# The gated linear attention of a hybrid decoder layer: from 32-token chunks to 128-token chunks by block levels

## The reference

```python
b = jnp.cumsum(gc, axis=1)                       # log decay, per token and key channel
diff = b[:, :, None] - b[:, None, :]
decay = jnp.exp(jnp.where(causal, diff, -jnp.inf))
att = jnp.einsum('bthd,bshd,btshd->bhts', qc, kc, decay)
o = einsum('bhts,bshv->bthv', att, vc) + einsum('bthd,bhdv->bthv', qc * exp(b), S)
S = S * exp(b_last)[..., None] + einsum('bshd,bshv->bhdv', kc * exp(b_last - b), vc)
```

## Time and profile before

| | us |
|---|---|
| median of three runs (lowest to highest) | 2495.36 (2492.14 to 2497.21) |
| the profiled execution's own time | 2494.72 |
| its span in the trace | 2492.9 |
| mean granted TensorE clock | 0.976 |

### The profile page before, as it was taken

The page is one execution under the profiler, slowest core; times in us unless marked ns, Lnnn a source line. Parts: engine busy times, 40 slices in busy tenths (PEclk is TensorE's granted clock), DMA queues, the critical chain, the costliest instruction groups (busy, mean ns, idle before and its releaser), DMA issues.

```text
span 2492.9 us, 47167 instructions
## 1 busy us (share of the span) xinstructions
PE 2452.3 (98%) x19106; PEld 2385.9 (96%) x19106; DVE 1360.8 (55%) x1555; ACT 989.3 (40%) x1037; POOL 162.2 (7%) x182
## 2 busy tenths in 40 slices
PE   8999999999999999999999999999999999999997
PEld 8999999999999998898888989999999999999997
DVE  6555554554556545544565465655555555555554
ACT  5333333333333334454455543444333333333332
POOL 0000000000004200010000130020000000000015
PEclk9999999999999999987898999999999999999998
DMA  5445445444444443251121544454445445445444
GB/s 210 168 152 185 168 157 182 168 167 167 183 170 151 176 163 131 102 192 69 67 81 71 188 176 169 169 185 170 184 164 191 184 166 189 183 167 189 184 166 139
DMA packets 67109, 401.72 MB, mean 161 GB/s; under 512 B 8706, under 2 KB 11426, under 8 KB 31696
## 3 DMA queue, kind: packets, MB, share of 16 engines
q1 hardware_dynamic: 62960, 386.86, 43.4%
q0 software_dynamic: 4080, 13.88, 1.6%
HBM read 391.43 MB, written 9.27 MB: 161 GB/s over the span
## 4 chain that ended last, share of the span: by engine, by line
PE 93%; DVE 2%; issue 2%; ACT 1%; POOL 1%; DMA 0%; DVEq 0%; SPq 0%; ACTq 0%; POOLq 0%
PE bank L1345 29%; PE bank L1351 29%; PE bank L1346 28%; PE bank L386 1%; PE bank L407 1%; PE bank L425 1%; ACT w_hi L618 1%; DVE w_lo L946 1%; PE bank L1479 0%; PE bank L423 0%; PE bank L370 0%; POOL scratch L596 0%; PE bank L1586 0%; PE bank L1477 0%; PE bank L1537 0%
## 5 line engine op out<-in xcount | busy, mean ns | idle before, releaser
L618 ACT ACTIVATE w_hi<-raw 128x2048 fp32r<-128x2048 f32 (+1 forms) x404 | 705.4, 1746 | 1238.0 <-PE bank L1351 1194.6
L946 DVE TENSOR_TENSOR w_lo<-raw,w_hi 128x2048 fp32r<-128x2048 f32 (+1 forms) x404 | 843.9, 2089 | 467.1 <-ACT w_hi L618 467.1
L1345 PE MATMUL bank<-x_hi,w_hi 128*128 128x264 f32 (+1 forms) x3440 | 898.9, 294 | 1.1 <-DVE x_lo L1289 1.1
L1346 PE MATMUL bank<-x_lo,w_hi 128*128 128x264 f32 (+1 forms) x3440 | 882.4, 289 | 0.0
L1345 PEld LDWEIGHTS bank<-x_hi,w_hi 128*128 128x128 f32 x3440 | 654.0, 190 | 21.4 <-issue 15.6
L1346 PEld LDWEIGHTS bank<-x_lo,w_hi 128*128 128x128 f32 x3440 | 653.8, 190 | 0.1
L1345 PE MATMUL bank<-y_hi,w_hi 128*128 128x264 f32 (+1 forms) x2368 | 598.1, 288 | 6.1 <-DVE y_lo L1248 5.6
L1346 PE MATMUL bank<-y_lo,w_hi 128*128 128x264 f32 (+1 forms) x2368 | 596.5, 287 | 0.0
L1351 PE MATMUL bank<-x_hi,w_lo 128*128 128x264 f32 (+1 forms) x3440 | 491.9, 293 | 0.0
L1351 PEld LDWEIGHTS bank<-x_hi,w_lo 128*128 128x128 f32 x3440 | 455.5, 191 | 4.0 <-issue 2.3
L1345 PEld LDWEIGHTS bank<-y_hi,w_hi 128*128 128x128 f32 x2368 | 447.1, 189 | 7.4 <-DVE y_lo L1248 6.9
(11 more groups left out here) (255 smaller groups left out, 1217.9 us busy)
## 6 DMA issues: line engine op xcount, KB each, us to landing
raw<-in_w_in SPq DMA_DIRECT2D x176, 1024.0 KB, 4.8
raw<-in_w_out SPq DMA_DIRECT2D x128, 704.0 KB, 4.0
raw<-in_w_proj SPq DMA_DIRECT2D x52, 1024.0 KB, 4.8
raw<-in_w_merge SPq DMA_DIRECT2D x32, 1024.0 KB, 4.9
raw<-in_w_o SPq DMA_DIRECT2D x16, 1024.0 KB, 4.8
scratch<-in_state_in POOLq DMA_DIRECT2D x8, 512.0 KB, 3.6
out_state_s<-scratch POOLq DMA_DIRECT2D x8, 512.0 KB, 4.8
hT<-in_xT SPq DMA_DIRECT2D x4, 560.0 KB, 7.2
```

What stands on the lines that cost most here:

```text
L618: act.activation(w_hi[:, b, 0:kt * P], raw[:, b, 0:kt * P], ACT.Copy).then_inc(hi_split, 1)
L946: dve.tensor_tensor(w_lo[:, b, 0:kt * P], raw[:, b, 0:kt * P], w_hi[:, b, 0:kt * P].bitcast(F32), ALU.subtract).then_inc(lo_split, 1)
L1345: pe.matmul(out, w, x[0][:, k, 0:T], start=(k == ks[0]), stop=False)
L1346: pe.matmul(out, w, x[1][:, k, 0:T], start=False, stop=False)
```

## The change

The chunk becomes 128 tokens, so there are two, and the decay inside is treated by seven block levels (h = 1, 2, 4 ... 64). At a level every second block of h queries is multiplied with the block of keys in front of it by one plain product per chunk and head (`level`, eight float32 matmuls with 64 columns), and the entries that belong to the level are picked out of PSUM by a copy under a mask (`pick_level`). Then late queries and early keys are scaled in place by the decay over a neighbouring block (`update`), so that after seven levels queries hold the decay from the chunk's start and keys that to its end. The decays of all block sizes are sums over pairs, one exponential for all. The diagonal comes from raw products (`raw_products`). The small matmuls of a slab stand in one run between its high pass and its low pass (`work_between`), for e = 8 to 20; outputs of a chunk stand in one run at e = 16 and e = 19. The loops over pairs of slabs are written out. Beside this, the z product takes 128 rows instead of 16, and at the end of the kernel POOL multiplies the final gains in as the tiles come, DVE squares the last tile, scales four tiles an instruction, and ACT issues two of the four stores.

PE before, inside the first slab of a pair: the outputs of a chunk stand between the matmuls of the high pass.

```diff
-CK = 16
+CK = 64
+LEVELS = 7
...
+        attT = at(3232, NCP * GH, CP)
+            pool.wait_ge(swa_pe, 4)
+            pool.memset(attT, 0.0).then_inc(att_zero, 1)
...
+            pool.wait_ge(z_done, 1)
+            pool.memset(k_meta, 0.0).then_inc(kx_zero, 1)
...
+            with pool.Fori(0, KD - 1) as m:
+                pool.wait_ge(bank_free, 2 * N_PAIRS - KD + m + 1)
+                pool.wait_ge(acc_done, 2 * KD + m)
+                h = hT[:, bass.ds(m, 1), 0:TR]
+                add_square(h, 2 * KD + m + 1, TR)
+                pool.tensor_tensor(h, h, gains[:, 3, bass.ds(m, 1)].unsqueeze(2).broadcast_to([P, 1, TR]),
+                                   ALU.mult).then_inc(y_gain, 1)
+            pool.wait_ge(rstd_done, 4)
+            pool.wait_ge(y_gain, KD - 1)
...
+                if e == 3:
+                    act.wait_ge(kx_zero, 1)
+                    act.wait_ge(g_log, 10)
+                    act.activation(table, table, ACT.Exp, scale=1.0 / TAU).then_inc(g_decay, 1)
+                    act.activation(spl, spl, ACT.Exp, scale=1.0 / TAU).then_inc(g_decay, 1)
...
+            def value_rows(n, q):
+                act.wait_ge(g_vt, 2 * n + q + 1)
+                if n:
+                    act.wait_ge(g_kv, n)
+                else:
+                    act.wait_ge(g_up, 2)
+                act.activation(v_rows[:, 512 * q:512 * q + 512], rows_bank(n, q)[:], ACT.Copy).then_inc(g_vtok, 1)
+            for e in range(8, 24):
                 act.wait_ge(bank_free, 2 * half + b + 1)
+                if e < 16:
+                    gate_a(half, slice(e, e + 1))
+                else:
+                    gate_r(e - 16)
+                if e == 10:
+                    for q in range(2):
+                        value_rows(0, q)
+                    key_rows(0)
+                if e in (13, 14):
+                    value_rows(1, e - 13)
+                if e == 15:
+                    key_rows(1)
+                if e == 16:
+                    out_tiles(0)
+                if e == 18:
+                    for q in range(2):
+                        value_rows(2, q)
+                    key_rows(2)
+                if e == 19:
+                    out_tiles(1)
...
+            for q in (1, 3):
+                act.wait_ge(y_done, q + 1)
+                if q == 3:
+                    act.wait_ge(y_last, 3)
+                act.dma_start(t["yT"][:, 4 * q:4 * q + 4, :], hT[:, 4 * q:4 * q + 4, 0:TR]).then_inc(y_out, 16)
...
+                if e == 7:
+                    dve.wait_ge(g_decay, 2)
+                    dve.wait_ge(g_att, 1)
+                    q = proj[:, GQ:GQ + GH, 0:NP_]
+                    dve.tensor_tensor(q, q, dec[1], ALU.mult).then_inc(g_qa, 1)
...
+            def update(i):
+                h = 2 ** i
+                dve.wait_ge(g_att, i + 2)
+                if i == 0:
+                    dve.wait_ge(g_qa, 1)
+                else:
+                    dve.wait_ge(g_up, 2 * i)
+                q = halves(proj[:, GQ:GQ + GH, 0:NP_], h, 1)
+                dve.tensor_tensor(q, q, by_block(dec[h], h, 0, NP_), ALU.mult).then_inc(g_up, 1)
+                k = halves(proj[:, GK:GK + GH, 0:NP_], h, 0)
+                dve.tensor_tensor(k, k, by_block(dec[h], h, 1, NP_), ALU.mult).then_inc(g_up, 1)
+            def pick_level(i):
+                h = 2 ** i
+                n = CK // h
+                dve.wait_ge(g_pick, i + 2)
+                m = mask(h).bitcast(mybir.dt.uint32).unsqueeze(1).unsqueeze(3).broadcast_to([P, NCP * GH, n, h])
+                dve.copy_predicated(halves(attT, h, 1), m,
+                                    bank[4 if i % 2 else 7][:].rearrange("p (g b x) -> p g b x", g=NCP * GH, b=n)).then_inc(g_pick, 1)
...
+            for e in range(8, 24):
+                half, b = GATE_A + e // 2, e % 2
                 dve.wait_ge(slab_done, 2 * half + b + 1)
+                dve.tensor_tensor(siga[:, e] if e < 16 else r_act[:], bank[b][:, 0:TR], rstd[:, 0:TR],
                                   ALU.mult).then_inc(bank_free, 1)
+                if e < 8 + LEVELS:
+                    update(e - 8)
+                split_lo(half + 1, b, KD)
+                if e == 8:
+                    dve.wait_ge(att_zero, 1)
+                    for c in range(NCP):
+                        pick_diagonal(c)
+                if e < 8 + LEVELS:
+                    pick_level(e - 8)
+                if e == 7 + LEVELS:
+                    dve.tensor_copy(a_chunk[:], dec[CP]).then_inc(g_chunk, 1)
+                if e in (12, 17, 20):
+                    new_state((12, 17, 20).index(e))
+                if e >= 16:
+                    silu_r(e - 16)
...
+            dve.wait_ge(y_gain, 12)
+            for q in range(3):
+                h = hT[:, 4 * q:4 * q + 4, 0:TR]
+                dve.tensor_tensor(h, h, rstd[:, 0:TR].unsqueeze(1).broadcast_to([P, 4, TR]), ALU.mult).then_inc(y_done, 1)
...
+                elif r == 3:
+                    pe.wait_ge(acc_done, KD * r - 1)
+                    pe.matmul(bank[7][:, 0:T], ones[:], acc[:, 0:T], start=True, stop=False)
+                    pe.wait_ge(last_sq, 1)
+                    pe.matmul(bank[7][:, 0:T], ones[:], act_a[:, 0:T], start=False, stop=True).then_inc(sumsq_done, 1)
...
+            def raw_products(i):
+                if i == KD - 1:
+                    for c in range(NCP):
+                        for h in range(GH):
+                            last = pe.matmul(bank[5 + c][:, h * CP:(h + 1) * CP], proj[:, GK + h, c * CP:(c + 1) * CP],
+                                             proj[:, GQ + h, c * CP:(c + 1) * CP], start=True, stop=True)
+                    last.then_inc(g_att, 1)
...
+            def level(i, n):
+                h, c, g = 2 ** i, n // GH, n % GH
+                if n == 0:
+                    if i == 0:
+                        pe.wait_ge(g_qa, 1)
+                    else:
+                        pe.wait_ge(g_up, 2 * i)
+                    if i >= 2:
+                        pe.wait_ge(g_pick, i + 1)
+                late = proj[:, GQ + g, c * CP:(c + 1) * CP].rearrange("p (b two x) -> p b two x", two=2, x=h)[:, :, 1]
+                last = pe.matmul(bank[4 if i % 2 else 7][:, n * CK:(n + 1) * CK].rearrange("p (b x) -> p b x", x=h),
+                                 proj[:, GK + g, c * CP:(c + 1) * CP], late, start=True, stop=True)
+                if n == 7:
+                    last.then_inc(g_att, 1)
+            def values_to_rows_of(n, j):
+                if j == 0:
+                    pe.wait_ge((g_pick, g_vtok, g_oT)[n], 2)
+                cols = slice(TA - P, TA) if n == 0 else slice((n - 1) * CP, n * CP)
+                last = pe.transpose(rows_bank(n, j // 4)[:, (j % 4) * P:(j % 4 + 1) * P], proj[:, GV + j, cols], ident[:])
+                if j % 4 == 3:
+                    last.then_inc(g_vt, 1)
+            def keys_to_rows(n, h):
+                if h == 0 and n == 0:
+                    pe.wait_ge(kx_up, 4)
+                    pe.wait_ge(swa_act, 10)
+                    pe.wait_ge(swa_dve, 12)
+                if h == 0 and n == 1:
+                    pe.wait_ge(g_up, 2 * LEVELS)
+                    pe.wait_ge(g_S, 2)
+                if h == 0 and n == 2:
+                    pe.wait_ge(g_ktok, 2)
+                k = k_meta[:, h] if n == 0 else proj[:, GK + h, (n - 1) * CP:n * CP]
+                last = pe.transpose(keys_bank(n)[:, h * DK:(h + 1) * DK], k, ident[:])
+                if h == GH - 1:
+                    last.then_inc(g_kt, 1)
+            def keys_by_values(n, h):
+                if h == 0:
+                    pe.wait_ge(g_ktok, n + 1)
+                    pe.wait_ge(g_vtok, 2 * n + 2)
+                    if n == 1:
+                        pe.wait_ge(g_S, 2)
+                        pe.wait_ge(g_pick, 2 + LEVELS)
+                    if n == 2:
+                        pe.wait_ge(g_S, 6)
+                last = pe.matmul(kv_bank(n, h // 2)[:, (h % 2) * DV:(h % 2 + 1) * DV], k_rows[:, h * DK:(h + 1) * DK],
+                                 v_rows[:, h * DV:(h + 1) * DV], start=True, stop=True)
+                if h == GH - 1:
+                    last.then_inc(g_kv, 1)
+            def outputs(c, n):
+                j, h, q = n // 2, n // 4, n // 2 % 2
+                out = o_bank(c, j // 4)[:, (j % 4) * CP:(j % 4 + 1) * CP]
+                if n == 0:
+                    pe.wait_ge(g_S, 2 + 4 * c)
+                    pe.wait_ge(g_pick, 2 + LEVELS)
+                    pe.wait_ge(g_up, 2 * LEVELS)
+                    pe.wait_ge(g_vtok, 4 + 2 * c)
+                if n % 2 == 0:
+                    pe.matmul(out, S[:, h, q * P:(q + 1) * P], proj[:, GQ + h, c * CP:(c + 1) * CP], start=True, stop=False)
+                else:
+                    last = pe.matmul(out, v_rows[:, j * P:(j + 1) * P], attT[:, GH * c + h], start=False, stop=True)
+                    if n == 15:
+                        last.then_inc(g_o, 1)
```

(35 more changed lines are left out.)

476 lines of the change are left out of this document (130 added, 346 removed).

## The result

The changed kernel takes 2381.11 us (median of four runs, 2378.76 to 2382.01) against 2494.55 for the kernel before beside it: ratio 0.954, 95% interval 0.953 to 0.956. The direction was right, and a size was wrong. Single executions of some kernels took far longer (2516 to 5820 us), at a lower clock or held up; they are left out of all times given here.

A forecast was written before the change was run, and what follows sets the result against it. PE was taken to bound the stage from decode to gate b; its terms sum to 167.0 us against 257.6, 90.6 less. With 4.0 off at the end and 0.64 added, 2494.72 becomes 2400.8, or 2401 us; range 2386 to 2422.

The forecast's parts named there:

- 56 matmuls of levels: PE's seven levels of eight float32 matmuls with 64 columns, priced at 0.33 us each: 18.5 us.
- switches: PE changing between slab matmuls and thirteen runs of small matmuls, there and back: 3.5 us.
- half clock: PE's clock at half behind the decode matmuls, 2.7 us lost, and as much for one further fall among the runs: 5.3.
- wait at e = 19: PE waits for the second chunk's values in rows, 6.3 us of steps against 3.9 of high pass: 2.4 us.
- wait ahead of gate b, with the transposes: Behind slab 23, PE has only eight transposes while gate b waits for splits, zeroing, copies and subtractions: 8.7 us.
- The rival of cheaper small matmuls: PE's 64-column float32 matmuls hide their weights and take 0.16 us; levels lose 9 us, outputs 3: 2389, chance 0.10.
- Ahead of the stage: Before e = 8: raw products of 2.4 us against 2.8 us of wait and transposes that go, counted as nothing.
- The end's 4.0: Kernel's end: reciprocal some 1.8 us earlier, scaling four tiles at once, stores from two queues: 4 us less, between 0 and 6.
- The clock did not fall behind the runs: Rival: the clock falls behind most of the 13 runs, 2.7 us each: +32, 2433, every third 2412; chance 0.15.
- ACT and DVE did not stretch the slabs: Rival: from e = 16 ACT and DVE bind, each of eight slabs ends 2 us later: 2417, chance 0.08.
- POOL's gain: POOL's third operation per tile, 0.6 us, fits with 0.5 to spare; rival: it is late, 4 us gone, 2405, chance 0.05.
- the three signs that were to show the forecast wrong: A level's run under 1.5 us, a clock under 0.9 over the stage, or PE waiting for DVE before a level.

The follow-up runs named there:

- experiments 1: Kernel after with levels, and the second matmul of each output pair, on 32 of 128 rows (parts of the sums left out): 2398.25 us in a single run.
- experiment 2: Kernel before with the second matmul of each output pair on 128 rows instead of 32 (left-over numbers in the added rows): 2454.22 us, ratio 0.984.
- experiment 4: Kernel after with matmuls of levels, outputs and keys by values scattered one by one among the low pass's matmuls: 2382.21 us, ratio 0.955.
- experiment 5: Kernel after with the product of the down-projected gate on 16 rows again instead of 128: 2383.88 us, ratio 0.956.
- experiment 7: Kernel after with work moved earlier against PE's two waits, in several versions; second chunk's values alone 2376.73 us, fastest version, which includes widened decode products, 2364.02.
- experiment 3: Kernel after with each level's product made twice, 56 more float32 matmuls of 64 columns: 2394.22 us, ratio to before 0.961.
- experiment 6: Kernel after with the meta tokens' decode products on 128 rows instead of 16, the added rows of the weights zeroed: 2376.79 us, ratio 0.953.

## Why the prediction was wrong

The place, the direction and the course were right: 257.6 us of the stage become 152.4, where the sum had 167.0. What I took for each term, and what it measured:

| term | predicted | measured |
|---|---|---|
| decode matmuls | 14.5 | 14.6 |
| sixteen slabs | 93.6 | 93.6 (taken over) |
| 56 matmuls of levels | 18.5 | 12.0 |
| 36 transposes | 4.3 | 3.5 |
| 12 keys by values | 6.6 | 4.7 |
| 32 outputs (at full clock) | 9.6 | 7.0 |
| switches | 3.5 | 1.5 (what is left) |
| half clock | 5.3 | 4.3 |
| wait at e = 19 | 2.4 | 2.4 |
| wait ahead of gate b, with the transposes | 8.7 | 8.9 |

(The measured ones are from start to start; the outputs' 8.7 us are split at 1.7 lost to the clock. The slab intervals are 100.1 together: 93.6 is taken over from the prediction, since low passes at e = 21 to 23 start 5.87 us apart against 5.85; the wait and 2.6 of half clock behind decode go off, and the 1.5 at the switches is what is left, not measured by itself.)

Of the 19.7 us by which 2400.8 was too high, 14.6 lie in the stage, 3.4 ahead of it and 0.5 behind it; 1.2 are the 0.64 added at the end and the 0.58 by which the profiled execution lies above the median.

**The step that failed** is "The rows are 0.30 us at 128 columns and 0.34 at 32, so these are not paid by the column; I take 0.33". The inference was right for 64 and 128 columns (0.21 and 0.22), the price wrong. The second row stands at a change from 128 to 32 rows, and experiments 1 and 2 show what such a change costs. The first row was not dear at all, it was read over too short a stretch: it is a product with 128 columns in front of one with 16, and in the trace of before the weight loads of the two start 0.23 us apart, close to the 0.21 and 0.22 of a run:

```profile
953.33 0.30 PEld L1456 LDWEIGHTS bank<-proj 64*128 64x128 f32 x2
953.56 0.30 PEld L1457 LDWEIGHTS bank<-proj 64*128 64x128 f32 x2
```

From matmul to matmul the wide one shows 0.30, and the narrow ones in front of it 0.14 (953.22 to 953.36). Nor does going from one half of the array to the other make these products dear: just before, two wide ones, one on each half, take 0.33 together and two narrow ones 0.14:

```profile
952.89 0.50 PE L1456 MATMUL bank<-proj 64*128 64x128 f32 x4
953.22 0.30 PE L1457 MATMUL bank<-proj 64*128 64x16 f32 x4
```

That part of my theory falls. I had looked for the nearest row by shape, and should have asked what stood in front of it and behind it. A row nearer to a level stood in the same trace, 16 float32 products with 64 columns on 128 rows in a run:

```profile
1163.07 1.97 PE L386 MATMUL bank<-scratch,band 128*32 128x64 f32 x32 [1.07 <-DVE scratch L343]
1164.88 0.35 PE L395 MATMUL bank<-hT 128*16 128x16 f32 x8
```

These are 0.11 us each (1.81 for 16), 57 ns an instruction. Their weights have 32 columns, so it is no price for a level, but it speaks against the sentence that no row shows float32 matmuls on 128 rows at 81 ns an instruction, and it would have set a lower bound far under 0.33.

Levels, outputs, keys by values and transposes are 11.8 of the 14.6 us. **The switches** had their price from the same kind of row; experiment 4 shows that there is next to none. The rival of cheaper small matmuls came nearest (2389), and its mechanism, weights loaded beside the product in front, is what the PEld view shows. It had the levels at 0.16 and thus too cheap, took 3 us off the outputs, and left the other terms as they were. The Trainium skill (TensorE: Matmul & The Clock Gate, Back-to-back issue gap) gave 81 ns for a sustained matmul with 128 columns; the float32 instructions here take 106 ns with 64 columns and 111 with 128, between that figure and my rows.

**Ahead of the stage** I had counted nothing, and 3.4 us came: the raw products cost 1.70 instead of 2.4, by the same wrong price, against the 2.8 that went; and the product on 128 instead of 16 rows, which my working did not mention, saved 0.4 us and, with 3.4 us of half clock, 1.7 more (experiment 5).

**The waits** were right to 0.2 us, in part by luck. The steps named (1.92, 2.29 and three of 0.43) add up to 5.5 us, not to "about 5.2"; and of the gate's three steps one runs beside split_lo, so that from the start of split_hi to the first copy it is 4.95 (1227.50 to 1232.45). The end's 4.0 measured 4.06, with the reciprocal 1.75 us earlier (1.8 predicted) and the first store 4.2 us sooner (4).

**The rivals.** The clock did not fall behind the runs, apart from the second outputs, which follow a wait (with the wait gone it did not fall there, experiment 7); the second fall of 2.7 us in the sum was a guess without a place, and 1.7 came. ACT and DVE did not stretch the slabs, 5.87 us apart at e = 21 to 23 and with room at the levels (experiment 3), apart from the two waits. POOL's gain ended before the next tile's square (2358.32 against 2358.90). The masked copies take 0.88 us against the 0.67 I took, hidden as was expected. Of the three signs that were to show the forecast wrong none came (a level 1.70 us, the clock 0.92, no wait for DVE in front of a level): they were set too far out to catch a miss of this size.

How the 67 us that experiment 2 does not explain (105.2 less 38) divide between fewer instructions and the rest of the clock was not taken apart. The windows bear on it: 0.92 of 152.4 us is about 24 us at half, 0.86 of 257.6 about 72, so that the clock gave back some 24 us in all.

## What to carry to other kernels

Before a price is taken from a row, look at what ran ahead of it and behind it, and take it over a whole repeat; PEld shows whether the weights were loaded ahead. Here a small float32 matmul whose weights have the shape of its neighbour's costs about 0.21 us in a run with 64 or 128 columns, one that changes the rows 0.1 to 0.2 more. Padding a small product with zeros to the rows of its neighbours cost nothing in experiment 6 and can be tried in an old kernel without any new algorithm. A wait on several things is only named by its last one: when that is moved, expect the next (here pick, state update, order behind the gate).

## What the runs showed that I had not expected

- Changing between 128 and 32 rows costs 0.19 us a matmul with 128 columns (0.41 against 0.22), between 128 and 16 rows 0.10 with 8 columns (0.32 against 0.22); 32 rows without a change cost 0.24 against 0.21. At a change the weight load starts with its product (0.01 us ahead) instead of 0.10 us ahead.
- Float32 and slab matmuls can alternate for some 0.02 us each (0.23 against 0.21).
- The clock was low without idle time on PE: PE was busy for 230.3 of the 231.4 us of the kernel before's pairs, at 0.89; with 64 products widened from 32 to 128 rows they were at 0.99.
